# Prompt attention: GpSimd scales the second head group's probabilities, VectorE the first group's

## The reference, cut to what matters

```python
s_s = einsum('bqghd,bqgkld->bqghkl', qrg, ks) * scale       # selected branch
p_s = softmax(where(tok_ok, s_s, NEG_INF))
o_s = einsum('bqghkl,bqgkld->bqghd', p_s, vs)
s_w = einsum('bqghd,bwgd->bqghw', qrg, kw) * scale          # window branch
p_w = softmax(where(w_ok, s_w, NEG_INF))
o_w = einsum('bqghw,bwgd->bqghd', p_w, vw)
o = g[..., 0:1] * o_c + g[..., 1:2] * o_s + g[..., 2:3] * o_w
```

## Time and profile before

| | |
|---|---|
| median of 3 runs | 831.82 us (830.76 to 832.16) |
| profiled execution, its own time | 829.77 us |
| span of the profiled execution, first to last instruction | 828.0 us |
| mean granted TensorE clock | 0.983 |
| busy: PE, DVE, ACT, POOL | 774.4, 375.8, 220.5, 166.9 us |

### The profile page before, as it was taken

How to read it: one execution, slowest core, us unless ns; L and a number is a source line. 1 busy time by engine, 2 the same in 40 slices (tenths; PEclk the granted TensorE clock), 3 DMA queues, 4 the chain that set the end, 5 groups by cost and what they waited for, 6 DMA issues and landing times.

```text
span 828.0 us, 11541 instructions
## 1 busy us (share of the span) xinstructions
PE 774.4 (94%) x4479; PEld 541.6 (65%) x4479; DVE 375.8 (45%) x799; ACT 220.5 (27%) x480; POOL 166.9 (20%) x270
## 2 busy tenths in 40 slices
PE   5999999997999999999999999999999899998763
PEld 3657778876766667777767777774456855555431
DVE  2201899999778880111006552231227632222106
ACT  3000324252256662233125640000001112221113
POOL 2338447100200006000005420002000213222010
PEclk9999999998999999999999999999999999999889
DMA  9676445130270005152214529703105999999847
GB/s 314 166 15 189 140 102 159 45 112 1 68 277 2 2 2 180 51 179 76 77 51 132 177 89 297 288 1 115 51 26 208 385 386 413 406 405 395 322 149 263
DMA packets 87505, 138.98 MB, mean 168 GB/s; under 512 B 25493, under 2 KB 60465, under 8 KB 86287
## 3 DMA queue, kind: packets, MB, share of 16 engines
q1 hardware_dynamic: 71439, 101.41, 35.7%
q0 software_dynamic: 11392, 32.71, 13.3%
q10 hardware_dynamic: 4616, 4.08, 1.6%
HBM read 132.00 MB, written 21.14 MB: 185 GB/s over the span
## 4 chain that ended last, share of the span: by engine, by line
PE 79%; DMA 8%; DVE 7%; issue 4%; SPq 1%; ACT 1%; ACTq 0%; POOL 0%; DVEq 0%; POOLq 0%
PE ps L1914 17%; PE ps L2099 15%; PE ps L2357 7%; PE ps L2435 6%; PE ps L1938 5%; PE ps L2012 4%; PE ps L2451 3%; DMA mgT<-w_up 2%; PE ps L2142 2%; PE ps L2117 2%; DVE cv L1399 2%; PE ps L2130 2%; DMA arena<-w_up 2%; DMA arena<-yscratch 2%; PE ps L2425 1%
## 5 line engine op out<-in xcount | busy, mean ns | idle before, releaser
L2099 PE MATMUL ps<-xT,keep 128*128 128x288 f32 x512 | 126.9, 408 | 0.8 <-ACT h L1210 0.5
L2099 PEld LDWEIGHTS ps<-xT,keep 128*128 128x128 f32 x512 | 96.7, 190 | 27.2 <-ACT h L1210 0.9
L1914 PE MATMUL ps<-xT,arena 128*128 128x288 f32 x384 | 95.4, 408 | 0.6 <-DVE keep L1492 0.6
L1914 PEld LDWEIGHTS ps<-xT,arena 128*128 128x128 f32 x384 | 72.3, 190 | 20.0 <-issue 0.8
L1399 DVE SCALAR_TENSOR_TENSOR cv<-keep,cv 128x512 f32<-128x512 f32 x120 | 83.7, 749 | 1.4
L2357 PE MATMUL ps<-arena,xT 128*128 128x512 f32 x128 | 55.4, 592 | 0.0
L2435 PE MATMUL ps<-keep,mgT 128*64 128x256 f32 x224 | 42.9, 396 | 2.1 <-DMA mgT<-w_up 2.1
L1938 PE MATMUL ps<-mgT,xT 128*128 128x512 f32 (+1 forms) x128 | 44.4, 507 | 0.0
L2357 PEld LDWEIGHTS ps<-arena,xT 128*128 128x128 f32 x128 | 24.2, 190 | 29.2 <-issue 29.1
L842 ACT ACTIVATE mgT<-ps 64x512 f32<-64x512 f32 x56 | 33.1, 591 | 32.3 <-PE ps L1992 31.7
L1280 ACT ACTIVATE keep<-h 128x1024 f32<-128x1024 f32 (+1 forms) x5 | 5.3, 1057 | 130.1 <-DVE h L1705 121.5
(11 more groups left out here) (409 smaller groups left out, 1337.7 us busy)
## 6 DMA issues: line engine op xcount, KB each, us to landing
arena<-w_down SPq DMA_DIRECT2D x19, 512.0 KB, 16.7
keep<-w_in SPq DMA_DIRECT2D x16, 512.0 KB, 3.9
arena<-w_gate SPq DMA_DIRECT2D x15, 512.0 KB, 8.6
arena<-w_up SPq DMA_DIRECT2D x15, 512.0 KB, 12.2
keep<-w_gate SPq DMA_DIRECT2D x14, 512.0 KB, 11.5
keep<-w_up SPq DMA_DIRECT2D x14, 512.0 KB, 17.0
h<-x_prompt SPq DMA_DIRECT2D x8, 512.0 KB, 5.2
arena<-w_in SPq DMA_DIRECT2D x8, 512.0 KB, 8.0
```

Source lines behind the costliest of these rows:

```text
L1914: last = mm(tokens(j)[:, b, :], weights(k), halves(x[:, k, :])[:, b, :], start=k == 0, stop=k == n_k - 1)
L2099: last = mm(out[:, 0:half], wmg[n // 2 % 3][:, k, :], xT[:, k, (n % 2) * half:(n % 2 + 1) * half], start=k == 0, stop=k == KD - 1, skip_gr ...
```

## The change

The scaling of step 4 is split by head group. VectorE still makes the factors and scales group 0. GpSimd scales group 1: a new loop over the 24 units stands in its list ahead of the wait on line 999. The semaphore `s_pn` becomes two, one for each group. GpSimd starts a unit once VectorE has finished the first scaling instruction of that unit (which comes after the factors), and TensorE waits for each group's own semaphore.

```diff
-        s_pn = sem("s_pn")
+        s_pn = [sem(f"s_pn{g}") for g in range(2)]
...
+                self.normed_to = sum(len(x[2]) for x in units[:u + 1])
...
+            def normalize(u):
+                x = unit[u]
+                pool.wait_ge(s_pn[0], x.normed_to - x.n_br + 1)
+                for b in range(x.n_br):
+                    k = slice(b * x.nk, (b + 1) * x.nk)
+                    nc.gpsimd.tensor_scalar(x.prob[:, 1, k], x.prob[:, 1, k], x.stat(3)[:, 1, b:b + 1], None, ALU.mult).then_inc(s_pn[1], 1)
+
+            for u in range(NU):
+                normalize(u)
             pool.wait_ge(s_pv, NU)
...
-                for g in range(NKV):
-                    for b in range(x.n_br):
-                        k = slice(b * x.nk, (b + 1) * x.nk)
-                        V.tensor_scalar(x.prob[:, g, k], x.prob[:, g, k], x.stat(3)[:, g, b:b + 1], None, ALU.mult).then_inc(s_pn, 1)
+                for b in range(x.n_br):
+                    k = slice(b * x.nk, (b + 1) * x.nk)
+                    V.tensor_scalar(x.prob[:, 0, k], x.prob[:, 0, k], x.stat(3)[:, 0, b:b + 1], None, ALU.mult).then_inc(s_pn[0], 1)
...
                 for g in range(NKV):
-                    pe.wait_ge(s_pn, x.exps_to - (NKV - 1 - g) * x.n_br)
+                    pe.wait_ge(s_pn[g], x.normed_to)
```

## The result

The changed kernel took 835.72 us (median of 20 runs, 831.96 to 840.3) against 832.22 (20 runs, 829.31 to 834.69) for the kernel before on the same chip. The ratio is 1.0042, with an interval of 1.0026 to 1.0057: slower, by more than the 0.2% that can be told. The profiled execution took 831.96, its span 830.1 at a clock of 0.985, so 2.19 above the one before (829.77, clock 0.983).

What follows compares the result with a forecast made beforehand. TensorE bounds the attention, with holes behind VectorE's copy. Winning 0.07 us in second and 0.35 in fifth units of four head pairs gives 1.7 us, taking the median from 831.82 to 830.1; range 827.9 to 836.6.

Steps and rivals of the forecast that it cites:

- the price that the prediction had set aside: GpSimd's scaling priced from L984, 2.8 ns a column, 1.70 us for 512 columns; it would give 837.1 us.
- GpSimd is the new bound: Rival: group 1's transposes in second and fifth units wait longer for GpSimd than for the copy; 835 us, chance 0.29.
- What bounds the kernel: Prompt attention: TensorE is the bound, waiting for VectorE's copy in second and fifth units; ceiling of the change 3.6 us.
- The copy comes earlier: VectorE's copy, freed of group 1's scalings, comes 0.53 us earlier in second units and 0.40 in fifth units.
- GpSimd's price: GpSimd's group 1 scaling in the attention: 1.25 ns a column, 0.43 to 0.91 us for 128 to 512 columns.
- The way to TensorE: From GpSimd's end to TensorE's group 1 transposes: 0.15 us, as the rows showed behind VectorE.
- The sum: Attention: 0.07 us won in each second unit and 0.35 in each fifth, over four head pairs 1.7 us.
- The break-even: GpSimd's price at which second-unit and fifth-unit effects cancel: 1.66 ns a column; chance of lying below it 0.56.
- The lock: Rival: GpSimd holds VectorE's copy out of shared ports until its scalings finish; 5.8 us lost, 837.6 us, chance 0.05.
- The page's price: GpSimd's scaling priced from the skill's 1.8 cycles an element: 1.04 us for 512 columns, a sum of about 0.8 us.
- Lost in the experts: Rival: the 1.7 us won in the attention is waited off at the experts' w_up loads; 831.8 us, chance 0.10.

Runs made afterwards that it cites:

- e2: The changed kernel with the scaling of group 1 left out, a ceiling only: 829.39 us, ratio 0.9960 to the kernel before; attention 76.66 us.
- e4: The kernel before with VectorE's list reordered to scaling of group 0, copy, scaling of group 1, without GpSimd: 829.23 us, ratio 0.9965; attention 77.01 us.
- e1: The kernel before with extra timed GpSimd instructions on a spare buffer, behind the preparation of the sample queries: 836.06 us, single run; attention 80.35 us.
- e5: The changed kernel with GpSimd's scaling written as a two-tensor product with the factor spread out: 832.17 us, ratio 0.9984 to the kernel before; attention 78.12 us.
- e8: The kernel before with VectorE's list as in e4, and GpSimd scaling group 1 only in third, fourth and sixth units: 829.73 us, ratio 0.9976.
- e9: The kernel before with VectorE's copy moved ahead of the whole scaling of the next unit, GpSimd not used: 831.18 us, ratio 0.9980.
- e10: The kernel of e4 run once more on another chip, against the kernel before: 829.49 us, ratio 0.9960; attention 77.03 us.
- e7: The kernel before with TensorE multiplying the previous unit's values between the transposes of group 0 and group 1: 839.3 us, one run; attention 85.85 us.
- e6: The kernel before with GpSimd also running scalings of the same widths on a spare buffer, nobody waiting: 836.43 us, single run; attention 81.21 us.

## Why the prediction was wrong

The direction was wrong: 830.1 and "faster" with 0.40, where the median is 835.72. It lies inside the range (827.9 to 836.6), whose upper end came from the price that the prediction had set aside, and in the rival called "GpSimd is the new bound", which had 0.29, said 835 and names what happened. Step by step:

- **What bounds the kernel.** Right. The holes were at the second and fifth units and came from the copy behind the scaling. e2 gives 3.71 us for the ceiling of 3.6; e4 takes 3.36 of it by the order alone.
- **The copy comes earlier.** Right in both places (0.49 gone, 0.76 down to 0.36). VectorE's busy time fell by 9.6 us against the 10.6 said.
- **GpSimd's price. This step failed**: the term was chosen as 0.43, 0.59, 0.75 and 0.91 us for 128 to 512 columns, and measured 0.61, 0.94, 1.25 and 1.57. The lower slope came from two rows of 4 and 16 columns in int32 (L891, L892), carried 32 times beyond the larger of them. And they were misread: the kernel has them multiply by a constant and add a value per partition, so they are no scaling by a factor per partition. The row with the same operation, type and kind of factor was L984; its line gave 2.8 ns a column against 2.5 measured and 1.70 us against 1.57. I set it aside for its source pattern, which e1 shows to cost nothing. From 16 to 64 columns it was already (437 - 288) / 48 = 3.1 ns each. Whether int32 or the second operation plays a part as well was not tried.
- **The way to TensorE.** Put at 0.15, the measured way from GpSimd's end to the weight load is 0.05 (257.09 to 257.14). And GpSimd began 0.09 after VectorE's first scaling, not after the second: the first ended at 254.79 + 0.35 = 255.14, the second at 255.41, and GpSimd was running from 255.23. Both errors made the forecast's gain smaller, by 0.10 and 0.23 us in the second unit, so they aren't why it was wrong.
- **The sum.** With the measured durations and 0.05 the prediction's own lines give 256.07 + 1.88 + 0.05 = 258.00 against 257.47 and 267.29 + 1.57 + 0.05 = 268.91 against 268.70: 4 x 0.74 = 3.0 us lost. The stage lost 2.60. With GpSimd's true start as well (0.09 behind VectorE's first scaling) they give 257.75 and 268.94, 4 x 0.52 = 2.1 lost. So the frame held to about 0.5 us either way, and one number in it did not. The break-even of 1.66 ns a column, too: e5, with 0.63 for 256 and 1.04 for 512 columns, lies on the good side of it (2 x 0.63 - 1.25 = 0.01 against 1.26 - 1.04 = 0.22) and came out ahead in the stage, by 2.25 us. The same lines with 0.05 for the way give it 0.09 in the second unit and 0.32 in the fifth, 4 x 0.41 = 1.6 us. So with the later start they are 0.6 us too dear there and 0.4 in the changed kernel.
- **The lock.** As a rival (the copy held by GpSimd) it was wrong: the copy L1542 started at 255.32 beside a running GpSimd and took its usual 0.42. Between scalings it is there. In three places of the changed kernel (one is at 268.37) a scaling of VectorE that started late in a GpSimd instruction took 0.52 us instead of 0.48. In the last unit VectorE started a scaling at 309.84 beside a GpSimd instruction that ended at 310.29, and took 0.73 us instead of 0.48:

```profile
308.73 1.56 POOL L1005 TENSOR_SCALAR arena<-arena 128x512 f32<-128x512 f32 x1 [1.78 <-DVE arena L1535]
309.84 0.73 DVE L1535 TENSOR_SCALAR arena<-arena 128x512 f32<-128x512 f32 x1
```

The Trainium skill (SBUF — State Buffer, Who interferes with whom) has one engine shut out while the other holds the shared ports, and leaves out of it a VectorE instruction with at most one SBUF input outside the 2-port modes, as this copy from PSUM is. The copy at 255.32 and the scaling at 309.84, which ended 0.28 after GpSimd's, fit. The first 512-column scaling of e1 doesn't: it ran from 335.80 to 337.36, VectorE's two-input instruction began inside it at 336.47, and both took their usual times (1562 and 759 ns). What the lock cost in the changed kernel is small, since GpSimd's mean durations there stay within 20 ns of the quiet ones.

- **The page's price.** The Trainium skill (GPSIMD Engine Reference, 3.1 Elementwise) has 1.8 cycles an element at best, which I had as an estimate of 1.04 us for 512 columns. That is what the product with a spread-out factor took (1.04), but by chance: its slope is 1.67 ns a column over 0.19 us, the estimate's 1.5 over 0.27. The scaling took half as much again. By the prediction's own lines that estimate makes the sum 4 x (0.22 - 0.05) = 0.7 us and not 0.8.
- **Lost in the experts.** Not seen: in all five runs whose stage became shorter by 3 us or more (e2, e4, e8, e9, e10) the whole was faster. How much of the stage's gain arrives can't be told closer than the intervals (0.3%, 2.5 us wide); e9, 3.01 shorter in the stage, has 0.8 by its medians and 0.2 to 3.1 by its interval, so a part lost isn't excluded.

Open: the 0.35 us between e4 and e2, and why the whole of the changed kernel lost 3.5 by its medians where the stage lost 2.60; the interval of the ratio (2.2 to 4.7 us) covers that.

## What to carry to other kernels

When an idle engine is offered work, find the row with the same operation, type and kind of operand, reading in the code what the row's instruction does, and trust its slope over that of rows closer in layout but far smaller in size. If the break-even lies between two candidates, the nearest in operation decides. Before moving work to another engine, ask what the wait is really for: here it was one copy standing behind work that nobody needed yet, and moving it up in the same list brought 0.4% without a second engine. An order changed on the engine that is the bound has its price as well, through whoever stands behind its later half (e7: 5.5 us).

## What the runs showed of the hardware that was not expected

- On GpSimd a two-input product with the factor spread out is cheaper than the scaling by a factor per partition: 400, 630, 826 and 1040 ns against 607, 939, 1246 and 1566 for 128 to 512 columns. With a constant factor the scaling took 1490, so the factor's source is not what makes it slow.
- Scalings of the two engines that overlap lengthen each other, in the clearest cases the one that comes second: GpSimd by 0.17 us in e6's fifth unit, VectorE by 0.24 in the changed kernel's last unit. The prediction had a price for two-input instructions only the earlier trace rows, and one such overlap in e1 cost neither engine anything.
- The attention's length in a trace repeated to 0.02 us where it could be compared (77.01 and 77.03 on two chips, 80.37 and 80.35), while the twelve whole times of e4 and of e10 lie 6.4 and 4.3 us apart. For a change inside one stage the trace's own length of it is the sharper measure, and the whole only confirms its sign.
